# Convolution tiles first in the projections, one ring of weights, whole-row taps in pairs of tiles, and modulations computed as columns

## What is computed

```python
mod = silu(c) @ ada_w + ada_b                 # 6 * 1024 values: shift1, scale1, gate1, shift2, scale2, gate2
u1 = layer_norm(x) * (1 + sc1) + sh1
proj = u1 @ w_in                              # RWKV r, k, v, lora | conv halves a, b | gates a, b
p_rw = p + mu_prev * (p_prev - p) + mu_next * (p_next - p)     # for r, k, v, lora
h = h_a * sigmoid(h_b)
h = depthwise_conv_31(h) + conv_b
h = silu(layer_norm(h, cnorm_w, cnorm_b))
y_b = (h @ cpw_w + cpw_b) * sigmoid(p_gate_b + gate_b)
```

## Time and profile before

| | us |
|---|---|
| median of 3 runs (2155.03 to 2160.31) | 2157.51 |
| the profiled execution | 2165.9 |
| its span | 2164.2 |
| PE busy in it | 1928.5 (89%) |
| DVE busy | 1399.5 (65%) |
| ACT busy | 880.3 (41%) |
| POOL busy | 660.9 (31%) |

### The profile page before, as it was taken

How to read it: one execution, slowest core, us unless ns; L and a number is a source line. 1 busy time by engine, 2 the same in 40 slices (tenths; PEclk the granted TensorE clock), 3 DMA queues, 4 the chain that set the end, 5 groups by cost and what they waited for, 6 DMA issues and landing times. The chain is left out here.

```text
span 2164.2 us, 54389 instructions
## 1 busy us (share of the span) xinstructions
PE 1928.5 (89%) x20438; PEld 1424.8 (66%) x20438; DVE 1399.5 (65%) x2791; ACT 880.3 (41%) x1464; POOL 660.9 (31%) x533
## 2 busy tenths in 40 slices
PE   5699999978399999999997788999999999999966
PEld 1576777746298998999894355666666666666632
DVE  2688788844254656565642847777777777777717
ACT  0322232222245454555431005555555555555501
POOL 4545444301534344434410301221122222122213
PEclk9899999989599999999998888999999999999988
DMA  5644554214200010001005118899889888888845
GB/s 198 209 132 145 179 167 151 80 53 132 70 21 10 17 32 26 26 14 32 14 14 189 65 51 342 325 344 328 329 323 337 314 318 328 315 326 326 319 168 215
DMA packets 161938, 377.90 MB, mean 175 GB/s; under 512 B 23572, under 2 KB 97474, under 8 KB 134385
## 3 DMA queue, kind: packets, MB, share of 16 engines
q1 hardware_dynamic: 140292, 337.50, 43.6%
q0 software_dynamic: 21152, 37.80, 4.9%
q10 hardware_dynamic: 335, 0.22, 0.0%
HBM read 361.00 MB, written 53.24 MB: 191 GB/s over the span
## 5 line engine op out<-in xcount | busy, mean ns | idle before, releaser
L1991 DVE TENSOR_TENSOR moe_w_lo<-moe_raw,moe_w_hi 128x1024 fp32r<-128x1024 f32 x272 | 315.0, 1221 | 2.5 <-ACT moe_w_hi L1910 2.1
L1910 ACT ACTIVATE moe_w_hi<-moe_raw 128x1024 fp32r<-128x1024 f32 x272 | 265.3, 1047 | 85.8 <-DMA moe_raw<-in_exp_up 83.9
L1854 PE MATMUL moe_pH<-moe_w_hi,moe_x_hi 128*128 128x512 f32 x544 | 221.1, 406 | 38.7 <-DVE moe_x_lo L1998 29.4
L1788 POOL DMA_INDIRECT moe_xg<-scratch_u2d,moe_idx x70 | 70.9, 1012 | 588.5 <-issue 513.4
L1864 PE MATMUL moe_pY<-moe_wd,moe_hT 128*128 128x512 f32 x544 | 244.8, 593 | 0.5 <-ACT moe_hT L1925 0.5
L419 POOL TENSOR_TENSOR proj_w_lo<-proj_w,proj_w_hi 128x1024 fp32r<-128x1024 f32 x59 | 177.2, 3008 | 211.3 <-ACT proj_w_hi L503 211.3
L621 DVE SCALAR_TENSOR_TENSOR proj_hc<-proj_hp,cwT,proj_hc 128x256 f32 x480 | 232.3, 557 | 7.9 <-DVE proj_st L594 7.9
L446 PE MATMUL proj_bank<-proj_u_hi,proj_w_hi 128*128 128x512 f32 x536 | 211.9, 395 | 24.5 <-DVE proj_u_lo L652 12.2
L1854 PE MATMUL moe_pH<-moe_w_hi,moe_x_lo 128*128 128x512 f32 x544 | 213.8, 393 | 0.0
L1854 PE MATMUL moe_pH<-moe_w_lo,moe_x_hi 128*128 128x512 f32 x544 | 213.5, 393 | 0.0
L446 PE MATMUL proj_bank<-proj_u_hi,proj_w_lo 128*128 128x512 f32 x536 | 210.6, 393 | 0.0
(11 more groups left out here) (337 smaller groups left out, 3679.5 us busy)
## 6 DMA issues: line engine op xcount, KB each, us to landing
moe_raw<-in_exp_gate SPq DMA_DIRECT2D x69, 1024.0 KB, 7.0
moe_raw<-in_exp_up SPq DMA_DIRECT2D x69, 1024.0 KB, 10.0
moe_wd<-in_exp_down SPq DMA_DIRECT2D x68, 1024.0 KB
proj_w<-in_w_in SPq DMA_DIRECT2D x59, 512.0 KB, 4.6
proj_aw<-in_ada_w SPq DMA_DIRECT2D x8, 2048.0 KB, 8.2
last_yb<-scratch_ybuf SPq DMA_DIRECT2D x4, 2560.0 KB, 25.0
mod_aw<-in_ada_w SPq DMA_DIRECT2D x4, 2048.0 KB, 19.6
scratch_rkv<-proj_st SPq DMA_DIRECT2D x24, 256.0 KB, 2.2
```

Source lines behind the costliest of these rows:

```text
L1788: pool.indirect_dma_start(out=xg[q][:], out_offset=None, in_=g["u2d"][:], in_offset=bass.IndirectOffsetOnAxis(ap=idx[q][:, 0:1], axis=0), ...
L1854: ins = nc.tensor.matmul(pH[:], a[:, k], w[p][:, k].rearrange("p w f -> p (w f)"), start=(k == 0 and n == 0), stop=(k == KC - 1 and n == 2))
L1910: nc.scalar.activation(w_hi[p][:, ks].rearrange("p k w f -> p w k f"), raw[p][:, :, ks], ACT.Copy) \
L1991: nc.vector.tensor_tensor(w_lo[p][:, ks].rearrange("p k w f -> p w k f"), raw[p][:, :, ks], w_hi[p][:, ks].rearrange("p k w f -> p w k f") ...
```

## The change

- The groups of `ada_w` become the stationary operand and `csil` the moving one, so that a modulation comes out as columns (one column of 128 for 8 matmuls). The first two modulations then need no way through DRAM; the other four are turned by one transpose and written once. Half of the columns (shift and scale of 4 chunks) are done before the first transposes of `x`.
- The splitting of `u1` into high and low parts moves into the first stage, which also preloads 5 weight tiles and splits the first of them.
- The second stage is unrolled. Its tiles stand in one list: 16 of the convolution, 8 of gate a, 8 of gate b, then r, k, v, then lora, then the 8 pointwise ones. Weights go through one ring of 5 raw and 4 split buffers, results through 6 banks and 6 staging rows. DVE makes the low parts; POOL has no work left in this stage.
- Taps go over whole rows of 512, in turn on two tiles; `tap_plan` says how many follow each tile. The layer norm of the convolution is done between later tiles. Gate b stays in SBUF.
- The other modulations follow tiles 20, 23, ... 41.

```diff
@@ modulation_and_norm, PE
-            for n in range(NG):
-                pe.wait_ge(aw_in[n], 16)
-                for k in range(KC):
-                    ins = nc.tensor.matmul(acc[n][0:1, :], g["csil"][:, k:k + 1], aw[:, n, k], start=(k == 0), stop=(k == KC - 1))
...
+            pe.wait_ge(rows_read, 7)
+            for h in range(2):
+                for n in (h, 2 + h):
+                    pe.wait_ge(aw_in[n], 16)
+                    for m in range(GROUP // P):
+                        col = (n // 2) * 4 + m
+                        for k in range(KC):
+                            ins = nc.tensor.matmul(acc[h][:, col:col + 1], aw[:, n, k, m * P:(m + 1) * P], g["csil"][:, k:k + 1],
+                                                   start=(k == 0), stop=(k == KC - 1))
                 ins.then_inc(mod_done, 1)
...
+                for k in range(4 * h, 4 * h + 4):
+                    if k >= 4:
+                        pe.wait_ge(tp_used, k - 3)
+                    turn(k)
@@ modulation_and_norm, ACT
+            for k in range(KC):
+                act.wait_ge(tp_used, k + 1)
+                nc.scalar.activation(g["u_hi"][:, k], u1[:, k], ACT.Copy).then_inc(tp_high, 1)
+            act.wait_ge(w_pre, 16 * RAW)
+            for n in range(SPLIT):
+                nc.scalar.activation(g["w_hi"][:, n], g["w"][:, n], ACT.Copy).then_inc(w_high, 1)
@@ the list of tiles and the plan of the taps
+TILES = [(kind, i) for i in range(KC) for kind in ("hb", "ha")] \
+    + [("ga", i) for i in range(KC)] + [("gb", i) for i in range(KC)] \
+    + [(kind, i) for i in range(KC) for kind in RKV] + [("lora", j) for j in range(3)]
+N_U = len(TILES)
+TILES += [("cpw", n) for n in range(KC)]
+RAW, SPLIT, BANKS_P, N_ST = 5, 4, 6, 6
+MOD_AFTER = list(range(20, 44, 3))
...
+    work = {"ha": 0.7, "r": 1.7, "k": 1.7, "v": 1.7, "lora": 1.7}
+    quota, ends, credit, done = [], [], 0.0, 0
+    for n in range(N_U):
+        credit += 5.45 + (3.6 if n in MOD_AFTER else 0.0) - 1.3 - (work.get(TILES[n - 1][0], 0.0) if n else 2.5)
+        there = 2 * CW * (n // 4)
+        q = max(0, min(int(credit / 0.67), there - done, KC * CW - done))
@@ projections_and_conv, PE
+            def modulate(c):
+                pe.wait_ge(aw_at[c % 2], 16 * (c // 2 + 1))
+                for m in range(MC):
+                    col = c * MC + m
+                    for k in range(KC):
+                        ins = nc.tensor.matmul(pmod[:, col:col + 1], aw[:, c % 2, k, m * P:(m + 1) * P], g["csil"][:, k:k + 1],
+                                               start=(k == 0), stop=(k == KC - 1))
+                ins.then_inc(S["mod_done"], 1)
...
+            for n in range(N):
+                product(n)
+                for q in range(KC // 2):
+                    if n == ends[q] + 1:
+                        mean(q)
+                if n in MOD_AFTER:
+                    modulate(MOD_AFTER.index(n))
+                if n == MOD_AFTER[-1] + 2:
+                    pe.wait_ge(S["modc_done"], 1)
+                    nc.tensor.transpose(pmod[0:KC * MC, P:2 * P], modc[:], g["ident"][:]).then_inc(S["turned"], 1)
+                if n == E_CONV + 3:
+                    variance()
@@ projections_and_conv, DVE
+            for n in range(N + 1):
+                if n == N_U:
+                    split_h()
+                if n >= 1:
+                    evict(n - 1)
+                if SPLIT <= n + 3 < N:
+                    low(n + 3)
+                if n < N_U:
+                    taps(quota[n])
...
+                if n == E_CONV + 2:
+                    centre()
+                if n == E_CONV + 4:
+                    v.wait_ge(S["std_done"], 1)
+                    nc.vector.reciprocal(rs[:], rs[:]).then_inc(S["rs_done"], 1)
+                if n == E_CONV + 5:
+                    normal()
```

More of the change, by code:

```diff
@@ L284, in _ @@
                                         ALU.subtract, ALU.mult).then_inc(xn_done, 1)
[L285 to L295, removed]
@@ L338, in projections_and_conv @@
[L338 to L345, removed]
@@ new lines, in _ @@
+            sp.dma_start(brow[:], ada_b[0, 2 * D:].rearrange("(r p) -> r p", p=P)).then_inc(S["brow_in"], 16)
+            for n in range(RAW, N + RAW + 3):
+                if n < N:
+                    load(n)
+                if n == RAW + 2:
+                    load_mod(0)
+                if n == RAW + 4:
+                    load_mod(1)
+                m = n - RAW - 3
+                if m in slot_of:
+                    store(m)
+                if m in MOD_AFTER and MOD_AFTER.index(m) + 2 < KC:
+                    load_mod(MOD_AFTER.index(m) + 2)
+                if m == N_U:
+                    sp.wait_ge(S["mrow_done"], 1)
+                    sp.dma_start(g["mod"][0, 2 * D:].rearrange("(r p) -> r p", p=P), mrow[:]).then_inc(S["mod_out"], 16)
@@ L441, in _ @@
+            for slot in range(N_ST):
+                sp.wait_ge(stored[slot], 16 * len([n for n in keeps if slot_of[n][0] == slot]))
+            sp.wait_ge(S["mod_out"], 16)
         @block.tensor
         def _(pe):
-            def product(o, j, k):
-                for n, (a, b) in enumerate(((w_hi, u_hi), (w_lo, u_hi), (w_hi, u_lo))):
-                    ins = nc.tensor.matmul(o[:], a[:, j, k], b[:, k], start=(k == 0 and n == 0),
-                                           stop=(k == KC - 1 and n == 2))
-                return ins
@@ new lines, in high_h @@
+            def high_h():
+                act.wait_ge(S["tile_done"], N_U)
+                for k in range(KC):
+                    act.wait_ge(S["silu"], k + 1)
+                    nc.scalar.activation(u_hi[:, k], hc[:, k], ACT.Copy).then_inc(S["h_high"], 1)
+            for n in range(N):
+                if n == N_U:
+                    high_h()
+                if n >= 1:
+                    evict(n - 1)
+                if SPLIT <= n + 3 < N:
+                    high(n + 3)
+                if n == E_CONV + 2:
+                    squares()
+                if n == E_CONV + 4:
+                    root()
+                if n == E_CONV + 6:
+                    silu(range(4))
+                if n == E_CONV + 7:
+                    silu(range(4, KC))
@@ L643, in conv_low @@
[L643 to L663 removed]
+            ch = Chain(v, S["taps"])
```

552 lines of the change are left out of this document (237 added, 315 removed).

## The result

The changed kernel took 2202.91 us, the median of 4 runs (2196.59 to 2211.22), against 2158.91 (2155.03 to 2161.20) for the kernel before on the same chip: a ratio of 1.0193, 95% interval 1.0169 to 1.0218. It is 44 us slower; the forecast was 2204 us. The profiled execution took 2211.22 us.

The account below looks back on a forecast made before the run. PE alone was taken to set the loop's pace. 2165.9 + 18 (first stage) - 20 (second stage) + 49 (clock in slices) = 2213 us profiled, 2204 us by the median; range 2152 to 2223.

Parts of the forecast that it names:

- Price of a column matmul: Modulation matmuls: 64 weight loads a slice at the trace's 0.11 us each, not the skill's estimated 5.2 us a slice.
- First stage, +18: Column matmuls and transposes at the half clock: first product matmul at about 91.6 us instead of 73.47.
- The tail: First stage behind PE's end at 85.5 us: eviction 0.75, high part 0.5, weight high parts 3.9, barrier about 0.9.
- Second stage without the clock, -20: Projection tiles: layer norm waits and half-clock losses removed, 1.5 us and about 0.5 added; sum -20 us.
- the two waits of 4.96 and 12.17 us: PE's idle times in the convolution's layer norm, behind the loop; the forecast had both removed.
- 1.5 us ahead of the pointwise tiles: Second stage, behind the last lora tile: one high and one low part before the first pointwise matmul, 1.5 us added.
- The clock in the slices, +49: Second stage's eight slices: clock falls after 3.0 us, rises after 4.9 of dense matmuls; 6.15 us each, +49.
- DVE costs nothing: Second stage: DVE's low parts, taps and other work stay hidden beside PE, so PE doesn't see them.
- The sum of 328 against 394: Second stage: DVE's work of 328 us against PE's 394, taken as cover.
- The rest, 0: Kernel from 538 us on, behind the last pointwise tile: untouched, unchanged length.
- B: Second stage: the clock falls in no slice; 2155 us, no change; chance 0.10.
- C: Both stages: continuous weight loads keep the clock up; 2126 us by the median; chance 0.11.

Follow-up runs that it names:

- e1: Changed kernel, second stage's modulation slices streaming 128 equal columns past each weight load instead of one: 2161.07 us, ratio 0.9979.
- e3: Changed kernel, second stage's modulation slices streaming 64 equal columns past each weight load instead of one: 2158.82 us, ratio 0.9974.
- e4: Changed kernel, second stage's modulation slices as rows of 512 columns again, first stage left as changed: 2156.48 us, ratio 0.9962.
- e5: Changed kernel, second stage's one-column matmuls spread, one behind every second product matmul of tiles 20 to 43: 2162.50 us, ratio 0.9986.
- e7: Changed kernel without the second stage's eight modulation slices, weight loads kept, bias alone stored: 2096.67 us, ratio 0.9679.
- e9: Kernel before, only the loop's eight row slices made one-column matmuls, all 512 values of each stored: 2203.05 us, ratio 1.0188.
- e10: Changed kernel, 128 equal columns in the first stage's modulation matmuls alone, one-column slices kept in the second: 2184.85 us, ratio 1.0092.
- e2: Changed kernel, 128 equal columns instead of one in both stages' modulation matmuls: 2132.58 us, ratio 0.9851.

## Why the prediction was right

- **Price of a column matmul.** Held: 0.213 us at the half clock, 0.110 at the full, in the changed kernel itself. From a slice's start to the next tile's are 7.06 us in e1 and e3. By the figure of the Trainium skill, TensorE: Matmul & The Clock Gate, section Back-to-back issue gap, it would be an estimated 5.2; the traces decide for 7.06. At the full clock slices by columns and by rows (6.96 in e4) cost the same.
- **First stage, +18: measured +20.05.** The column matmuls came out right (54.5 us, forecast 54.6); PE ended at 85.9 instead of 85.5. The tail was mis-sized, 7.6 us of PE's wait instead of 6.1: DVE alternates evictions with low parts, 1.32 us a chunk, so the last chunk's high part and the four weight high parts behind it start later (the last of them ends at 92.67). The +20 is one of two cases. The same code had its first product matmul at 93.5 us here and in e5, but at 89.7 to 90.5, +16 to +17, in e1, e3, e4 and e7, where the clock was up for a while in the middle (see the last section). The forecast had it down throughout.
- **Second stage without the clock, -20: measured -25 to -26.** 483.2 us against 464.1 is +19; less the 44 to 45 of the slices, -25 to -26; e1, without falls, has -25.1. The terms that the sum had are there: the two waits of 4.96 and 12.17 us are gone, and 1.5 us ahead of the pointwise tiles has come. By the starts of PE's instructions it left out three things: the 2.5 us in which PE did not work in the loop, which stood in rows that I had read the earlier trace rows; a first rise of the clock that came 4.26 instead of 6.2 us after the start, 1.0; and the statistics of the layer norm, where mean and variance together take 11.74 us between the tiles against 17.06 before, waits left out, 5.3 less, of which the sum had 3.3 (the half clock in the variance). They make 5.5, against the 5 to 6 that are missing.
- **The clock in the slices, +49: measured +45.** Mean fall after 3.39 us (forecast 3.0), mean rise after 4.51 (4.9). e1, e3, e4 and e5 show that it goes when the streaming is there, e9 that it comes without the rest of the change.
- **DVE costs nothing.** Held for the changed kernel, where PE never waits for it but for the 1.5 us forecast: a tap is 0.68 us of DVE's time (162.2 us for 240), under the 0.75 taken. e7 shows how thin the cover is: without 56 us of slices PE waits 8.6 us for it. The sum of 328 against 394 did not say so, since it averages over tiles with and without taps.
- **The rest, 0: measured +6.2** in the two profiled executions (1632.8 against 1626.6 us). In the runs here with 34 blocks the same code takes 1621 to 1634 us, and I have no cause for the difference. Of the 6.2 us, 2.6 are there when the expert stage's first matmul starts, and 3.5 come from there to the last stage's first matmul, which takes 794 to 804 us in the ten traces with 34 blocks (796.7 before, 800.2 in the changed kernel). e10, the other one with dips and this order, has the longest, and 1633.8 for the rest. It stays open whether that is chance.
- **Rivals.** B (no fall) and C (loads keep the clock) fall by the rows above: PE was busy without a gap in the slices, loads running all the time, and the clock fell. The Trainium skill, TensorE: Matmul & The Clock Gate, section What's actually happening, read as how busy PE is, would have it stay up. D didn't happen.
- **A reading that was off.** The clock of the page of before is below 9 tenths in the second of the 40 parts as well as around the ninth to eleventh. Nothing in the sum rests on it.

In all +20 -26 +45 +6 (or -25 with 44 for the slices) is +45 in the profile, 44 by the medians. The mechanism was right; that the number came within 2 us is partly luck, since the errors of +2, -6, -4 and +6 cancel.

## What to carry to other kernels

Turning a matmul round so that the result comes in columns saves no PE time where the weight loads set the pace, and where it makes PE stream almost nothing for some microseconds it costs the clock, in that stretch and in the dense one behind it. Keep such matmuls wide, if need be with equal columns that nobody reads, or put them singly between dense ones; either kept the clock at 1.00 here and gave back some 40 to 46 us (e1, e3, e5). And when a run leaves work out or stores wrong values, count the work of everything that depends on the data before reading its time.

## What was not expected of the hardware

- With 64 columns a matmul the clock stayed at 1.00 in e3, where it had been 1.00 before. L1551, with 64 columns and the loads just as dense, stayed at 0.50 for 13 us in the kernel before, and with 128 columns in e2 the clock came up from the half within 5 us. Whether holding and raising differ, or something else about L1551, no run here tells.
- Extra columns were free up to the loads' pace: the next tile starts 7.06 us after the slice with 64 and with 128, and 64 instructions at 0.11 are 7.0.
- The clock could rise in the middle of the first stage, and in identical code it did in some executions and not in others. In e1, e3, e4 and e7 its first records are 1.00, from 2.9 to 4.2 us after the 16 f32 transposes between the halves began, and the second half of the column matmuls took 24.2 to 24.5 us instead of 27.30; in the changed kernel and e5 it did not rise. That the transposes' own columns raised it is likely but not shown. In e1 it was 1.00 from 55.9 to 59.3 us:

```profile
51.75 3.65 PE L238 MATMUL mod_tp<-ident,mod_x 128*128 128x128 f32 x16
55.20 24.20 PE L255 MATMUL mod_acc<-csil,mod_aw 128*128 128x1 f32 x128
```
